# Attention 1 between the chunks of the convolution's projection, and the modulation's products packed into fewer layers

## The reference

```python
h = concatenate([meta, x])                      # 16 + 256 = 272 tokens
z = rmsnorm(h, norm_mix) @ w_in                 # q, k, v: 8 heads of 128; gate_b, gate_c, hc: 1024 each; 8 forget logits
attn = softmax(q k' * scale + c_q - c_k + causal) v       # c: running sum of log_sigmoid(forget)
conv = gate_b * short_conv(gate_c * hc, conv_w)           # 3 taps over the tokens
y = rmsnorm over each of 16 groups of 128 of [attn, conv] * out_gain
h = h + y @ w_out
h = h + swiglu(rmsnorm(h, norm_ffn))            # d_ff 5632
h = rmsnorm(h, final_norm)[16:]
# second block
mod = silu(c) @ w_mod + b_mod                   # 12288 values; the same for c_ctx, of which the first 4096 are used
# then a norm with scale and shift, three kinds of mixing (latent attention, neighbourhood attention, Fourier),
# a gated residual, and a convolutional feed-forward part
```

## Time and profile before

| | us |
|---|---|
| median of three runs | 2537.32 |
| profiled execution | 2559.61 |
| its span | 2557.6 |
| TensorE busy | 2455.5 |
| DVE busy | 1767.9 |
| ACT busy | 1196.3 |

### The profile page before, as it was taken

The page is one execution under the profiler, slowest core; times in us unless marked ns, Lnnn a source line. Parts: engine busy times, 40 slices in busy tenths (PEclk is TensorE's granted clock), DMA queues, the critical chain, the costliest instruction groups (busy, mean ns, idle before and its releaser), DMA issues.

```text
span 2557.6 us, 43456 instructions
## 1 busy us (share of the span) xinstructions
PE 2455.5 (96%) x14574; PEld 2145.6 (84%) x14574; DVE 1767.9 (69%) x2846; ACT 1196.3 (47%) x1718; POOL 0.2 (0%) x4
## 2 busy tenths in 40 slices
PE   7999999989999999999899999899999999999997
PEld 6989957978888888889877887568888888888886
DVE  6654435889878888888976434546777567766775
ACT  5344443456645664445522423344655444444453
POOL 0000000000000000000000000000000000000000
PEclk9999968999999999999989999999999999999999
DMA  7765503878867886787747521115455555555553
GB/s 274 257 206 174 181 16 146 288 255 284 276 241 258 275 283 244 249 283 268 277 162 277 193 75 50 66 68 187 140 189 195 189 181 190 183 193 183 188 189 124
DMA packets 140143, 508.65 MB, mean 199 GB/s; under 512 B 15392, under 2 KB 17440, under 8 KB 139552
## 3 DMA queue, kind: packets, MB, share of 16 engines
q1 hardware_dynamic: 140064, 507.61, 57.6%
HBM read 505.46 MB, written 2.10 MB: 198 GB/s over the span
## 4 chain that ended last, share of the span: by engine, by line
PE 85%; DVE 8%; DMA 3%; issue 2%; ACT 2%; DVEq 0%; SPq 0%; ACTq 0%
PE ps L862 40%; PE ps L864 19%; PE ps L887 5%; PE ps L886 5%; PE ps L888 5%; DMA wm<-in_mod_stream 2%; DVE lo L1273 2%; PE ps L1146 1%; PE ps L861 1%; DVE wm L1296 1%; PE ps L908 1%; DVE xnf L1357 1%; PE ps L909 1%; PE ps L910 1%; ACT hi L474 1%
## 5 line engine op out<-in xcount | busy, mean ns | idle before, releaser
L1273 DVE TENSOR_TENSOR lo<-raw,hi 128x1024 fp32r<-128x1024 f32 x754 | 917.0, 1223 | 544.7 <-ACT hi L474 542.4
L474 ACT ACTIVATE hi<-raw 128x1024 fp32r<-128x1024 f32 x754 | 796.3, 1060 | 855.9 <-PE ps L864 443.9
L862 PE MATMUL ps<-hs,hi 128*128 128x512 f32 x3008 | 1050.6, 396 | 11.2 <-DVE lo L1273 7.8
L864 PE MATMUL ps<-hs,lo 128*128 128x256 f32 x2820 | 798.4, 283 | 0.0
L862 PEld LDWEIGHTS ps<-hs,hi 128*128 128x128 f32 x3008 | 555.4, 189 | 128.9 <-DVE lo L1273 6.6
L864 PEld LDWEIGHTS ps<-hs,lo 128*128 128x128 f32 x2820 | 533.2, 189 | 8.6
L862 PE MATMUL ps<-hid,hi 128*128 128x512 f32 x1216 | 421.9, 394 | 0.0
L864 PE MATMUL ps<-hid,lo 128*128 128x256 f32 x1136 | 320.6, 282 | 0.0
L862 PEld LDWEIGHTS ps<-hid,hi 128*128 128x128 f32 x1216 | 223.1, 188 | 46.0
L1296 DVE SCALAR_TENSOR_TENSOR wm<-wm,cbx 128x1024 f32<-128x1024 f32 x192 | 234.0, 1220 | 9.2 <-DMA wm<-in_mod_stream 9.0
L886 PE MATMUL ps<-xs,hi 128*128 128x258 f32 (+1 forms) x784 | 226.4, 289 | 5.1 <-DVE lo L1273 2.7
(11 more groups left out here) (274 smaller groups left out, 2786.2 us busy)
## 6 DMA issues: line engine op xcount, KB each, us to landing
raw<-in_stream SPq DMA_DIRECT2D x754, 512.0 KB, 4.1
wm<-in_mod_stream SPq DMA_DIRECT2D x192, 512.0 KB, 4.4
h<-in_tokens SPq DMA_DIRECT2D x4, 544.0 KB, 5.2
cx<-in_ctx_tokens SPq DMA_DIRECT2D x1, 2048.0 KB, 9.8
out_tokens<-h SPq DMA_DIRECT2D x4, 512.0 KB, 3.0
cbx<-in_c_rows SPq DMA_DIRECT2D x1, 1024.0 KB, 12.2
cbc<-in_c_rows SPq DMA_DIRECT2D x1, 1024.0 KB, 4.5
na<-in_na_bias SPq DMA_DIRECT2D x1, 1024.0 KB, 4.9
```

What stands on the lines that cost most here:

```text
L474: act.activation(hi[:, slot, :], raw[:, slot, :], ACT.Copy).then_inc(hi_done, 1)
L862: ins = pe.matmul(both, hi[:, slot, w], pair, start=kt == 0, stop=kt == last_k)
L864: ins = pe.matmul(ps[:, bank, 0:NX], lo[:, slot, w], x_hi, start=False, stop=False)
L1273: dve.tensor_tensor(lo[:, slot, :], raw[:, slot, :], hi[:, slot, :].bitcast(F32), ALU.subtract)\
```

## The change

Attention 1 moves between the chunks of conv1. conv1 becomes one iteration of 12 halves, and its stream is put in another order: for two groups g, g+1 the halves are (gate_c, hc) of g, (gate_c, hc) of g+1, (gate_b of both). TensorE's list in half hf is `scores(hf)`, chunk 0, statistics of head hf-1, chunk 1, `transposed(hf)`, chunk 2, `mix(hf)`, chunk 3, for hf below 8. The product gate_c * hc and the one with gate_b are taken from PSUM by DVE (`conv_input`, `conv_output`) without a copy of all three through ACT. Group statistics are two products of 128x1 a group (`gstat`), with the squares as the stationary operand. The norms of groups 0 to 13 are spread in halves 9 to 11, the last two groups within out1, and out1's first eight chunks are in another order (`OUT_ORDER`), so that chunks on the first eight groups come first. The transposes of v go between q1's chunks. kv1 is written out instead of looped, the first silu moves behind the fourth split of kv1, and the products move:

| layer | products an iteration before | after |
|---|---|---|
| kv1 (2 iterations, 16 chunks each) | 8 | 12, chunks 4 to 15 |
| q1 (16) | 8 | 16 |
| conv1 (48) | 0 | 8, in the last four halves |
| out1 (32) | 12, and 4 of the context, up to chunk 30 | the same numbers, chunks 9 to 24 |
| dn1c (2 iterations, 12 chunks each) | 8 | 4, chunks 0, 2, 4, 6 |
| joint (2 iterations, 8 chunks each) | 16 | 8 |

`na` and `wfn` are loaded behind kr's weights instead of joint's, the second row of c (`cbc`) in conv1's half 9 instead of out1's start.

```diff
-LAYERS = ([Layer("kv1", 2, 4, 4, x_at=(0, 2, 4, 6, 8, 10, 12, 14)), Layer("f1", 1, 1, 2, tiles=1),
-           Layer("q1", 1, 4, 4, x_at=(0, 2, 4, 6, 8, 10, 12, 14)),
-           Layer("conv1", 3, 4, 4),
-           Layer("out1", 1, 8, 4, x_at=(1, 3, 5, 7, 9, 11, 13, 15, 17, 19, 21, 22), ctx_at=(24, 26, 28, 30))]
-          + ffn_layers("1", ((1, 4), (0, 5)), (1, 5), (0, 1, 3, 4, 6, 7, 9, 10))
-          + [Layer("joint", 2, 2, 4, x_at=(0, 0, 1, 1, 2, 2, 3, 3, 4, 4, 5, 5, 6, 6, 7, 7)), Layer("kr", 1, 1, 2, tiles=1),
+LAYERS = ([Layer("kv1", 2, 4, 4, loop=False, x_at=tuple(range(4, 16))), Layer("f1", 1, 1, 2, tiles=1),
+           Layer("q1", 1, 4, 4, x_at=tuple(range(16))),
+           Layer("conv1", 1, 12, 4, x_at=tuple(4 * _hf + _j for _hf in range(8, 12) for _j in (1, 2))),
+           Layer("out1", 1, 8, 4, x_at=(9, 10, 11, 13, 14, 15, 17, 18, 19, 21, 22, 23), ctx_at=(12, 16, 20, 24))]
+          + ffn_layers("1", ((1, 4), (0, 5)), (1, 5), (0, 2, 4, 6))
+          + [Layer("joint", 2, 2, 4, x_at=tuple(range(8))), Layer("kr", 1, 1, 2, tiles=1),
...
-                if ly.name == "joint":
+                if ly.name == "kr":
                     sp_.wait_ge(wm_used, MOD_CHUNKS + 2)
...
-            silu_rows(cbx, 0)
...
+            def first_silu(it, n):
+                if it == 0 and n == 3:
+                    silu_rows(cbx, 0)
+
+            to_z("kv1", 0, 0, after=first_silu)
...
+            def group_stats(g, squares):
+                for th in range(2):
+                    ins = pe.matmul(gstat(g)[:, th:th + 1], squares[:, th * P:th * P + P], mean[:, 0:1], start=True, stop=True)
+                return ins
...
+            def gn_spread(first, groups):
+                for g in range(first, first + groups):
+                    for th in range(2):
+                        ins = pe.matmul(gn_row(g)[:, th * P:th * P + P], ginv(g)[:, th:th + 1].to_broadcast([P, P]), ident,
+                                        start=True, stop=True)
...
+            for hf in range(LY["conv1"].halves):
+                if hf < HEADS:
+                    scores(hf)
+                conv_piece(hf, 0)
+                if 1 <= hf <= HEADS:
+                    head_stats(hf - 1)
+                if hf in (4, 7, 10):
+                    conv_stats(2 * (hf // 3) - 2)
+                if hf == 9:
+                    pe.wait_ge(gn_r, 1)
+                    gn_spread(0, 6)
...
+                conv_piece(hf, 1)
+                if hf < HEADS:
+                    transposed(hf)
+                conv_piece(hf, 2)
+                if hf < HEADS:
+                    mix(hf)
+                conv_piece(hf, 3)
...
+            for turn, (hf, j) in enumerate(OUT_ORDER):
+                out_piece(hf, j, turn)
+                if turn == 0:
+                    conv_stats(6)
+                if turn == 2:
+                    pe.wait_ge(gn_r, 3)
+                    gn_spread(14, 2)
...
+            for hf in range(conv.halves):
+                if hf >= 1:
+                    if conv_half(hf - 1)[0] == "u":
+                        conv_input(hf - 1)
+                    else:
+                        conv_output(hf - 1)
+                if hf < HEADS:
+                    masked(hf)
+                if hf >= 1:
+                    prepare(conv, 0, hf - 1, 3)
+                if hf < HEADS:
+                    inverse_sums(hf)
+                prepare(conv, 0, hf, 0, 1)
...
+                def first_two(it):
+                    gn_apply(8, 4)
+                    prepare(ly, it, 0, 0, 1)
+                    gn_rest(2)
+                    gn_inverse(2, 14, 2)
+                    prepare(ly, it, 0, 1, 2)
+                    gn_apply(12, 2)
+                    prepare(ly, it, 0, 2, 3)
+                    gn_apply(14, 2)
+                    gn_rest(3)
```

More of the change, by code:

```diff
@@ L559, in _, with take_v @@
             act.activation(fl[0:HEADS, 1, :], fl[0:HEADS, 2, :], ACT.Ln, bias=1.0).then_inc(f_act, 1)
-            to_z("q1", 16, NM - 2, SCALE1)
+            def take_v(it, n):
+                if n % 2 or n >= 12:
+                    return
+                i = n // 2
+                rows = P if i % 3 < 2 else N1 - 2 * P
+                act.wait_ge(vt_ready, i + 1)
+                act.activation(vtok[0:rows, i % 3, 512 * (i // 3):512 * (i // 3) + 512], ps[0:rows, 4 + i % 2, :],
+                               ACT.Copy).then_inc(vtok_ready, 1)
+            to_z("q1", 16, NM, SCALE1, after=take_v)
             def exps(hd):
@@ L612, in _ @@
[L612 to L621 removed]
+                act.activation(head_sq(hd), ps[:, 7, NX:2 * NX], ACT.Square).then_inc(y_ready, 1)
@@ new lines, in conv_squares, with gn_root @@
+            def conv_squares(hf):
+                kind, g = conv_half(hf)
+                if kind == "b":
+                    for t in range(2):
+                        act.wait_ge(bank_free, conv_freed(2 * hf + t + 1))
+                        act.activation(z[:, 40 + g + t, 0:NX], z[:, 24 + g + t, NM:N1], ACT.Square).then_inc(conv_sq, 1)
+            def gn_root(first, groups, stat):
+                act.wait_ge(*stat)
+                act.activation(gstd(first, groups), gstat(first, groups), ACT.Sqrt, bias=col("eps")).then_inc(gn_std, 1)
@@ L637, in body @@
                     for hf in range(ly.halves):
+                        if ly.name == "out1" and hf < 2:
+                            continue
                         prepare(ly, it, hf, 0, 1)
@@ L641, in body @@
                             after_first(it, hf)
+                        if ly.name == "out1" and hf == 2:
+                            squares(it, 0)
                         if sums and hf >= 1:
@@ new lines, in piece @@
+                slot = weights(ly, it, *((hf, j) if turn is None else (0, turn)))
+                for t in range(ly.tiles):
+                    bank = (2 * hf + t) % 4 if first_bank is None else first_bank + t
+                    if j == 0:
+                        pe.wait_ge(bank_free, ly.tbase + 2 * hf + t + 1 + it * ly.tpi)
+                    for k in range(kk):
+                        kt = j * kk + k
+                        if x_ready is not None and t == 0:
+                            pe.wait_ge(*x_ready(kt))
+                        w = slice(k * width + t * P, k * width + t * P + P)
+                        x_hi, x_lo = xs(kt)
+                        acc_ = ps[:, bank, 0:n]
+                        if len(x_hi.shape) == 3:
+                            acc_ = acc_.rearrange("p (a n) -> p a n", a=2)
+                        pe.matmul(acc_, hi[:, slot, w], x_hi, start=kt == 0, stop=False)
+                        pe.matmul(acc_, hi[:, slot, w], x_lo, start=False, stop=False)
+                        ins = pe.matmul(acc_, lo[:, slot, w], x_hi, start=False, stop=kt == last_k)
@@ L1014, in mix @@
                 ins.then_inc(o_ready, 1)
-            def group_stats(hd):
-                pe.wait_ge(gn_sq, hd + 1)
-                for a in range(2):
-                    e0 = TABS["e31"][0] + 15 - (8 * a + hd)
-                    ins = pe.matmul(ps[0:16, 1, 0:NX], tabs[:, e0:e0 + 16], gsq(hd)[:, a, :],
-                                    start=hd == 0 and a == 0, stop=hd == HEADS - 1 and a == 1)
-                ins.then_inc(gn_stat, 1)
-            scores(0)
-            to_z("conv1", NM - 2)
@@ L1546, in residual @@
                     dve.memset(sqb[:, 1, :, :], 0.0).then_inc(sum_added, 1)
+                if sums and ly.name != "out1":
+                    clear_sums()
                 run(dve, ly, body)
@@ L1943 @@
     w_in, w_in2 = a["w_in"][0], a["w_in_2"][0]
+    parts = {"b": 24, "c": 32, "h": 40}
+    tiles = [t for g in range(0, 8, 2) for t in (("c", g), ("h", g), ("c", g + 1), ("h", g + 1), ("b", g), ("b", g + 1))]
+    w_conv = np.concatenate([w_in[:, P * (parts[n] + g):P * (parts[n] + g + 1)] for n, g in tiles], 1)
+    w_out = chunks(a["w_out"][0])
+    w_out = np.concatenate([w_out[[4 * hf + j for hf, j in OUT_ORDER]], w_out[8:]])
     o = np.cumsum([0, 512, 512, 64, 512, 512, 512, 512])
```

393 lines of the change are left out of this document (226 added, 167 removed).

## The result

Four executions of the changed kernel took 2497.95 to 2504.04 us, median 2500.64; beside them the kernel before had 2537.43 (four executions, 2536.42 to 2548.24). The prediction said 2481 in 2468 to 2498: right in direction, 19.6 us too low, and outside its range by 2.6.

A forecast was written before the change was run, and what follows sets the result against it. TensorE, busy 96% of the span, was taken as the bound, at half clock in attention 1. Terms 43.3 + 1.8 - 5 - 1 + 1.4 + 5.8 + 9.2 = 55.5 us off 2537.3 gave 2481.8, say 2481; range 2468 to 2498.

The forecast's parts named there:

- Attention 1 into conv1: From q1's last matmul to out1's, 331.97 us become 288.7 with attention between conv1's chunks: gain 43.3 us.
- 286.7: TensorE's work in us from q1's last matmul to out1's at the 2.4 GHz level, before 2 us of waits.
- the ring: Weight loads in q1: a lead of three chunks (8.6 us, less 2.5 for a split) just covers falling 5 us behind.
- The heads: Heads in conv1 don't wait in themselves: 8.7 us of TensorE work covers 6.8 to 7.8 us beside it.
- The fourth rival: Clock falls in mid-conv1, eight head steps at 0.50 after a pause at head 0: 135 us more, 2616; chance 0.03.
- The first silu: At kv1's start DVE's first `lo` waits for the silu: pause 5.7 us, clock loss 2, together -5 us.
- +1.8: v's transposes between q1's pieces: the wait for `vtok`, the bias on DVE and two columns go; gain in us, at least +1.
- the -1 for packing: Packed products in kv1, q1 and out1 put DVE and loads slightly behind: -1 us, bounds 0 and -12.
- Ends of stages: With products moved away, waits shrink: out1's end to 3.9 us (+1.4), dn1c's to 5.3 (+5.8); joint's end gains +9.2.
- 5.8 + 9.2: Gains in us at dn1c's end (bounds +2 and +7) and at joint's end, `na` behind kr's loads (+6 and +10).
- The first rival: Product loads don't keep up in out1, q1 and kv1: 8 to 12 us lost in all, 2491; chance 0.14.

The follow-up runs named there:

- the version with the filled pause: Kernel before, with 24 fp32r products filling TensorE's 1.70 us pause between conv1's last chunk and the scores of head 1: 2535.74 us, ratio 0.9958.
- The less dense version: Changed kernel with 20, 8, 20 and 12 products in kv1, q1, conv1 and out1 instead of 24, 16, 8 and 12: 2495.84 us, ratio 0.9815.
- the version with the fill behind the pause: Kernel before, with 60 filling fp32r products behind the scores of head 1, so that the pause stays: 2548.02 us, ratio 1.001.

## Why the prediction was right and wrong

**The step that failed** is the second sentence of its first part: "differences are added up against the trace, and their sum comes off the median". The stretch of 47.7 us at 0.50 was read as a property of the kernel. It was a property of that execution: another had 23.9 us, and with the pause filled there is none. Taking it away was counted in full in the 43.3 us, half of 47.7 = 23.9; but the executions of the median had little or none of it. With no such stretch at all, and 1.3 us of fill more than the pause, the kernel takes 2535.7, and the median was 2537.3. Those three executions were not profiled, so this is inferred; it agrees with the mean clock, which is 0.979 to 0.981 in executions of 2533 to 2538 us and in the version with the filled pause, and 0.970 in the profiled one. The 22.3 us between profile and median were then for the most part this same stretch, and the prediction took them off a second time. The arithmetic: 22.3 us over the median before, 2.1 after, 20.2 of difference, less the 1.4 by which the profiled sum was short of the gain, is 18.8, the miss from 2481.8 to 2500.6. With the offset left out where the change removes its cause, the forecast was 2559.6 - 55.5 = 2504, which the prediction did name, for the profile.

That its sum of 55.5 came so near the 56.9 of the traces is luck in part. Attention 1 fell short by 5.9 us, and the start (1.6), out1's end to dn1c's (2.1), dn1c's end to the queries (1.0) and what lies behind them (2.4) gave 7.1 more than stood there.

The three executions shown before were also a low sample by chance. 70 later executions of the kernel before, 60 beside the experiments and the ten of its own run, go from 2528.8 to 2564.8 us with a median of 2545.7, quartiles 2537 and 2551. The changed kernel's ten have a median of 2501.9. So the change gains 44 us; against the kernel before with its clock held up in attention 1 (2535.7), it gains 34.

**Attention 1 into conv1**, 43.3 expected: from q1's last matmul (183.97 - 1.73 = 182.24) to out1's (480.50 - 3.72 = 476.78) it is 294.5 us, gain 37.4. The work was sized rightly: 294.5 less the waits (1.73 for `cq`, 0.66 at turn (0, 3), 2.4 for `lo` in out1) and 3.4 for 6.8 us at 0.50 is 286.3, where 286.7 stood. The waits were not. At head 0 the prediction saw the product that stands before `masked(0)`, but not that `cq`, which releases the scores, stands behind the products too. DVE at q1's end:

```profile
181.12 1.23 DVE L1397 TENSOR_TENSOR lo<-raw,hi 128x1024 fp32r<-128x1024 f32 x1 [1.01 <-ACT hi L513]
182.26 1.22 DVE L1420 SCALAR_TENSOR_TENSOR wm<-wm,cbx 128x1024 f32<-128x1024 f32 x1
...
183.66 0.17 DVE L1547 COPY cq<-ps 128x16 f32<-128x16 f32 x1
```

The arrears that the prediction granted q1 (5 us, covered by the ring) were there, and were no matter for the ring; they were one for a small copy that waits its turn behind them. The less dense version shows it: there `cq` is copied in time, and the wait is gone.

**The heads** waited nowhere, as predicted. The scores' line, with least, median and greatest ns, and first and last start:

```profile
L1086 PE MATMUL ps<-z x32: 390/393/498, 184.0 to 308.0; 128*128 128x272 f32 x32
```

124.0 us, less 1.5 within the last head and 3.4 at low clock, are seven steps of 17.0, where 16.9 stood. The fourth rival (the clock down for all of conv1) was wrong in its "once there": the pause at head 0 did come, 1.73 us, and the clock was back after 6.8 us, with products between the heads as in the version with the fill behind the pause.

**The first silu**: 5.68 us, predicted 5.7. Half of 6.8 us at 0.50 behind it is 3.4, predicted 2. Up to q1's last matmul the kernel is 2.6 us later than before (182.24 against 179.60), where -5, +1.8 and part of the -1 for packing gave 3.2 to 4.2.

**Ends of stages.** out1's pause is 3.72 (3.9 predicted), dn1c's 4.67 (5.3). From dn1c's end to the first wait of the queries' projection (behind `vt_m`, at 1552.9 us) it takes 321.5 us instead of 337.5, 16.0 gained where 5.8 + 9.2 = 15.0 stood. From out1's end to dn1c's it is 754.6 instead of 758.1, 3.5 gained for 1.4; and 2.4 came behind that wait, where nothing was predicted. Out1's pause is shorter by 1.6 us, which is part of the 3.5; where the rest and the 2.4 come from stays open. With 37.4 - 2.6 that makes the 56.7 between the two spans.

**The first rival**, loads that don't keep up, held in small: 2.4 us of waits for `lo` in out1, where DVE works 68.53 of 80.6 us. That DMA could carry it was right: it moved 410 GB/s at a share of 1.00 in 479.7 to 489.9. The figure that the Trainium skill gives for a core's share of HBM in "DMA: Bandwidth & Descriptors", Specifications, about 358 GB/s, is exceeded by that too. One core ran here; what a core gets while its neighbour loads as well, no run of this case shows.

## What to carry to other kernels

When a profiled execution lies far from the median, find what is slow in it before adding up differences: if the change removes just that, its price is in the offset already, and may be subtracted once. A stretch at half clock behind a short pause is a price of the pause, and its length can differ from execution to execution; filling or moving the pause shows what it costs. It costs half its length only where TensorE sets the pace in it. And where products are packed until an engine runs in arrears, look in its list for the small instructions behind them that release another engine.

## What the runs showed of the hardware

- A pause of TensorE of 1.70 us between dense projection and fp32 work was followed by 23.9 or 47.8 us at clock 0.50, 6.8 us when fp32r products came first, and none when the pause was filled (2.97 us of products).
- The same pause doesn't cost the same in every execution. Behind the 2.73 us for `lo` at kv1's start (37.64 us) the kernel before had no time at 0.50 in its first profiled execution and 3.4 us in its second; with the pause of attention 1 filled, which comes 290 us later, it was 6.8 us.
- Fill of fp32 products held the clock as well as fp32r ones: 2485.3 and 2485.5 us. So fp32 work held a clock that was up. That it doesn't raise one that is down as fp32r products do is what the runs on attention 1 suggest, where the clock stayed at 0.50 for 23.9 or 47.8 us of it; the reason stays open.
- With one core busy, DMA moved 410 GB/s at a share of 1.00 over 10.2 us.
